# Two layers of mixers, woven tighter: one level and one softmax unit a round, four projections as a fourth thread, a shorter opening

## What is computed

```python
h = rmsnorm_2(x, norm1_g[l]); u = h @ w_in[l]        # 3648 columns
(mq, mk, mv, mo, mi, mf, aq, ak, av, hq, hf, hi, hg) = jnp.split(u, split_at, axis=-1)
y_m = mlstm_mixer(...)       # 4 heads of 64: silu(conv(q, k)), exp-gated scores, / max(|den|, exp(-m)), norm, * sigmoid(mo)
y_a = diff_attention(...)    # 4 heads x 2: softmax(q0 k0) - lam * softmax(q1 k1), times v, norm
y_h = hgrn2_mixer(...)       # 4 heads of 64: gated linear attention with per-channel decay, norm, * silu(hg)
x = x + concat(y_m, y_a, y_h) @ w_out[l]
x = x + square(relu(rmsnorm_2(x, norm2_g[l]) @ w_up[l])) @ w_down[l]
```

## Time and profile before

| what | value |
|---|---|
| median of three runs | 2468.59 us |
| the profiled execution | 2469.0 us, its span 2467.2 us |
| PE / DVE / ACT busy | 93% / 64% / 56% of the span |
| chain that ended last | PE 66%, DVE 16%, ACT 11%, DMA 6% |
| granted PE clock, mean | 0.964 of 2.4 GHz |
| opening, then mixers, of the first such layer | 1650.7 to 1677.4 us, 1677.4 to 1842.7 us |
| the same of the second | 2062.7 to 2089.0 us, 2089.0 to 2253.0 us |

### The profile page before, as it was taken

The page is one execution under the profiler, slowest core; times in us unless marked ns, Lnnn a source line. Parts: engine busy times, 40 slices in busy tenths (PEclk is TensorE's granted clock), DMA queues, the critical chain, the costliest instruction groups (busy, mean ns, idle before and its releaser), DMA issues.

```text
span 2467.2 us, 38778 instructions
## 1 busy us (share of the span) xinstructions
PE 2291.2 (93%) x16290; PEld 2119.9 (86%) x16290; DVE 1577.4 (64%) x2235; ACT 1377.3 (56%) x1910; POOL 19.9 (1%) x14
## 2 busy tenths in 40 slices
PE   7989999999999899998999999999669999877999
PEld 6979998999999799997888888788559998756999
DVE  4666555666575665463888888867646665754765
ACT  5754546544566554554777777766444444654443
POOL 0000000000000000000000000000000000000000
PEclk9999999999999899997999999999879999988999
DMA  6531234555454213341888888954114564412453
GB/s 230 155 110 52 95 104 145 171 175 186 156 166 158 92 52 103 112 158 70 315 297 300 302 307 307 313 186 137 57 35 145 180 197 146 140 35 77 163 188 137
DMA packets 111205, 398.12 MB, mean 161 GB/s; under 512 B 12336, under 2 KB 12336, under 8 KB 110768
## 3 DMA queue, kind: packets, MB, share of 16 engines
q1 hardware_dynamic: 111024, 395.58, 48.1%
HBM read 394.48 MB, written 1.05 MB: 160 GB/s over the span
## 4 chain that ended last, share of the span: by engine, by line
PE 66%; DVE 16%; ACT 11%; DMA 6%; issue 2%; SPq 0%; DVEq 0%; ACTq 0%
PE ps L413 65%; DVE wlo L2008 7%; DMA raw<-stream 5%; ACT whi L1234 4%; ACT arena L1244 3%; DVE arena L2008 2%; DVE arena L2016 1%; DVE scr L2008 1%; ACT scr L1244 1%; ACT arena_r L1244 1%; DVE h L2008 1%; DMA CO<-const 1%; ACT L1244 1%; ACT rst L1244 1%; DVE scr L2016 0%
## 5 line engine op out<-in xcount | busy, mean ns | idle before, releaser
L2008 DVE TENSOR_TENSOR wlo<-raw,whi 128x1024 fp32r<-128x1024 f32 (+1 forms) x762 | 901.6, 1197 | 552.0 <-ACT whi L1234 542.2
L1234 ACT ACTIVATE whi<-raw 128x1024 fp32r<-128x1024 f32 (+1 forms) x762 | 781.3, 1035 | 347.3 <-PE ps L413 268.0
L413 PE MATMUL ps<-uh,whi 128*128 128x256 f32 (+1 forms) x2240 | 654.3, 292 | 13.9 <-ACT scr L1244 6.2
L413 PE MATMUL ps<-ul,whi 128*128 128x256 f32 (+1 forms) x2240 | 635.4, 284 | 0.0
L413 PE MATMUL ps<-uh,wlo 128*128 128x256 f32 (+1 forms) x2240 | 635.0, 284 | 0.0
L413 PE MATMUL ps<-arena_r,whi 128*128 128x256 f32 x2720 | 491.3, 283 | 19.7 <-DVE arena_r L2008 12.3
L413 PEld LDWEIGHTS ps<-uh,whi 128*128 128x128 f32 (+1 forms) x2240 | 429.7, 192 | 25.9 <-issue 17.4
L413 PEld LDWEIGHTS ps<-arena_r,whi 128*128 128x128 f32 x2720 | 420.0, 190 | 24.5 <-DVE arena_r L2008 13.4
L413 PEld LDWEIGHTS ps<-ul,whi 128*128 128x128 f32 (+1 forms) x2240 | 429.9, 192 | 6.0 <-issue 5.2
L413 PEld LDWEIGHTS ps<-uh,wlo 128*128 128x128 f32 (+1 forms) x2240 | 429.4, 192 | 0.0
L413 PE MATMUL ps<-arena_r,wlo 128*128 128x256 f32 x1360 | 381.9, 281 | 0.0
(11 more groups left out here) (163 smaller groups left out, 1902.5 us busy)
## 6 DMA issues: line engine op xcount, KB each, us to landing
raw<-stream SPq DMA_DIRECT2D x694, 512.0 KB, 4.1
raw<-stream SPq DMA_DIRECT2D x64, 384.0 KB, 4.2
CO<-const SPq DMA_DIRECT2D x1, 2305.0 KB, 13.2
h<-xT SPq DMA_DIRECT2D x1, 1024.0 KB, 5.8
raw<-stream SPq DMA_DIRECT2D x4, 256.0 KB, 2.6
out<-h SPq DMA_DIRECT2D x4, 256.0 KB, 2.2
arena<-pT SPq DMA_DIRECT2D x2, 256.0 KB, 3.9
SM<-small SPq DMA_DIRECT2D x1, 464.0 KB, 3.2
```

Of the source, the lines that this page charges most:

```text
L413: return self.e.matmul(o, l, r, start=start, stop=stop, skip_group_check=True)
L1234: self.e.activation(M.whi[:, b:b + n], M.raw[:, a:a + n], ACT.Copy).then_inc(K.sem("weight_hi"), 1)
L2008: return self.e.tensor_tensor(o, a, b, op)
```

## The change

1. **Opening.** `mv` and `hv` leave it. PE: three sums, one `av` piece, the fourth sum, two `av` pieces, `columns`, the last `av` piece. ACT and DVE call `ahead` four times fewer there; `odd_values` is gone.
2. **Filler thread**, first in every round, on all three engines, with PSUM bank 2 alone (`mlstm` keeps 0 and 1). It idles for 8 beats, then has one piece a beat: `hv` 8 and 9, `mv` 10 and 11, `mo` 12 and 13, `hg` 14 and 15. `hv` and `mv` now use `u1` (no scaling) and one bank for both token tiles.
3. **mlstm** starts two beats earlier and no longer holds `mo`. PE: gates 2, `mc` 4 to 7, `mac` and `mE` 8, `mE` 9, `ms` 10 and 11, `md`, `me`, `mn` 12, `fin` 14. ACT and DVE keep step.
4. **attention**: projections in 1 to 8 as before, `normed` in 4, 6, 8, 10; then `softmax_beats`: scores of units 0 to 3 in beats 11 to 14, transposes in 12 to 15 (after the next unit's scores), `ao` in 14 and 16, `fin` in 15 and 17. DVE has the maximum (`most`) in 11 to 14 and `shares` in 12 to 15, ACT the exponentials in 11 to 14: the same beats as PE.
5. **hgrn**: level -1 in beat 5, level n in beat 6+n on PE and DVE both (DVE: product n, merge n-1, difference for n+1), decays of n+1 on ACT in the same beat; `ho` 14, `fin` 15.

No product, sum or copy of the mixers is left out; only the scaling by the column goes. The last beat of a stage is 17 in place of 34. The core of the diff:

```diff
-MLSTM = 4
+MLSTM = 2
+FILL = 8
+def softmax_beats(result, steps):
+    units, norms = [(h, qt) for h in (0, 2) for qt in range(2)], []
+    for n in range(8):
+        for x in norms:
+            next(x, None)
+        if n in (3, 5):
+            norms.append(result(n - 3))
+            next(norms[-1])
+        for late, step in steps:
+            if 0 <= n - late < 4:
+                step(*units[n - late])
+        yield
 # Tensor
+    def filler(self, l):
+        work, s = self.ring((2,)), self.mark("tensor_filler")
+        yield from idle(FILL)
+        yield from self.pair_values(work, s, ("hv", l), "w_in_2", l, 3080)
+        yield from self.pair_values(work, s, ("mv", l), "w_in_2", l, 512)
+        yield from self.proj_T(work, s, ("mo", l), "w_in_2", l, 768, 256)
+        yield from self.proj_T(work, s, ("hg", l), "w_in_2", l, 3336, 256)
 # Tensor.opening
+        end = self.values(*end, end=True)
+        if not first:
+            next(end)
         self.wait_ge(self.K.sem("const"), 16)
         self.sums(tag, range(4) if start else (3,))
-        for n, _ in enumerate(self.values(*end, end=True)):
-            if n == 0:
-                self.columns(tag)
+        for _ in range(1 if first else 2):
+            next(end)
+        self.columns(tag)
+        for _ in end:
+            pass
 # Tensor.attention
-        for h in (0, 2):
-            yield from heads(h)
+        yield from softmax_beats(result, ((0, score), (1, turn)))
 # Scalar.attention: ((1, turned), (0, exps)); Vector.attention: ((1, shares), (0, most))
 # Tensor.hgrn
         for lev in range(8):
-            yield
-            yield
             self.wait_ge(*K.when("hqk", l, lev))
             ...
             yield
-            if lev == 3:
-                yield from self.proj_T(work, s, ("hg", l), "w_in_2", l, 3336, 256)
 # Vector.hgrn
-        scores(-1)
-        yield
             ...
             self.tt(v3(x, 512), v3(B["hqk"], 512), wide(E, 512, 2), MUL).then_inc(*s("hqk", l, lev))
+            scores(lev - 1)
             if lev < 7:
                 decays(lev + 1)
             yield
-            yield
-            if lev < 7:
-                scores(lev)
-            yield
 # Tensor, Scalar, Vector .layer_b
-        weave([self.mlstm(l), self.attention(l), self.hgrn(l)])
+        weave([self.filler(l), self.mlstm(l), self.attention(l), self.hgrn(l)])
```

More of the change, by code:

```diff
@@ L243, in weave, with idle @@
                 live.remove(th)
[L246 to L251, removed]
-            yield
+def idle(n):
+    for _ in range(n):
+        yield
[10 more added lines that the diff above has]
+                step(*units[n - late])
+        yield
 def beside(thread, other, k):
@@ L483, in values, with pair_values @@
             yield
+    def pair_values(self, work, s, tag, name, l, c0):
+        b = self.bank(work, *tag)
+        for k0 in (0, 4):
+            i, wt = self.piece(name, l, k0, 4, c0, T)
+            for t in range(2):
+                for k in range(4):
+                    self.wait_ge(*self.K.when(*self.u_ready(k0 + k)))
+                    last = self.mm3(b[:, t * T:(t + 1) * T], pick(self.U, ALL, k0 + k, slice(t * P, t * P + P)),
+                                    pick(wt, ALL, k, ALL), k0 + k + t == 0, k0 + k == 7)
+            last.then_inc(*s(("used", i), *([("ps", *tag)] if k0 else [])))
+            yield
     def sums(self, tag, qs):
@@ L1069, in mlstm @@
         b = self.bank(work, "mn", l)
-        for t in range(2):
-            self.wait_ge(*K.when("mv", l, t))
+        self.wait_ge(*K.when("mv", l))
         for pt in range(2):
@@ L1128, in heads, with turn, result @@
+        def turn(h, qt):
+            nk = (qt + 1) * P
+            b = self.bank(work, "at", l, h, qt)
+            for z in range(2):
+                self.wait_ge(*K.when("ap", l, h + z, qt))
+                for j in range(qt + 1):
+                    last = self.e.transpose(b[:, z * nk + j * P:z * nk + (j + 1) * P], pa[z][:, j * P:(j + 1) * P], M.ident)
+            last.then_inc(*s("ps", "at", l, h, qt))
+        def result(h):
             b = self.bank(work, "ao", l, h)
@@ L1798, in mlstm @@
         self.act(B["E"], B["E"], ACT.Exp).then_inc(*s("mE1", l))
[L1799 to L1806, removed]
+        yield from idle(3)
         x = self.take(scr, "mem", l)
@@ L1935, in hgrn @@
             yield
[L1936 to L1951, removed]
+        for z in range(2):
+            self.wait_ge(*K.when("ps", "hs", l, 7, z))
+            self.act(v3(B["ST"][:, z * 1024:(z + 1) * 1024], 512)[:, :, P:T], v3(self.bank("hs", l, 7, z))[:, :, 0:P],
+                     ACT.Copy).then_inc(*s(("hst", l, z), ("free", "hs", l, 7, z)))
         self.wait_ge(*K.when("ps", "ho", l))
@@ L2040, in opening @@
         K, M, s, U = self.K, self.M, self.main, self.M.U
-        for _ in range(4):
+        short = tag[0] == "n1"
+        for _ in range(1 if short else 4):
             self.ahead()
@@ L2062, in low @@
                     SUB).then_inc(*s(("u1", tag, q), ("free", "nu", tag, q), *([("free", "rs", tag)] if q == 3 else [])))
-        self.ahead()
+        for _ in range(2 if short else 1):
+            self.ahead()
         self.wait_ge(*K.when("rs", tag))
@@ L2070, in opening @@
         scaled(3)
[L2071 to L2074, removed]
+        for q in (1, 2):
+            if not short:
+                self.ahead()
+            low(q)
         low(3)
@@ L2812, in hgrn @@
+        yield from softmax_beats(lambda h: self.group_norm(s, l, 2 + h, 2, gs), ((1, shares), (0, most)))
     def hgrn(self, l):
```

218 lines of the change are left out of this document (98 added, 120 removed).

## The result

The changed kernel takes **2502.56 us** (median of four, 2500.11 to 2504.10), the kernel before 2467.82 (median of four on the same chip): ratio 1.0139, 95% interval 1.0126 to 1.0152. It is slower by 1.4%. The forecast was 2490, in a range of 2446 to 2510. The profiled execution took 2500.11, its span is 2498.2 against 2467.2: 31.0 us more.

The account below looks back on a forecast made before the run. Chains across engines, plus PE's half clock, bound the mixers. Per layer: opening -10.7, from the first `u1` product +20.7 (121 + 49 + 16 against 165.3), later resume 0.7; both layers +21.4 on 2469.0 gave 2490 us, range 2446 to 2510.

Parts of the forecast that it names:

- The mechanism: Mixers from beat 6: PE's level waits for DVE's same-beat product and merge, behind that beat's mlstm and attention steps.
- The waits, beat by beat: PE's waits in mixer beats 6 to 17, priced one by one: together 49 us of idle in place of 40.
- The clock: Half-rate PE after waits in the mixers: 16 us a layer lost in place of 15, bounds 8 and 25.
- The opening: Before the first `u1` product: four pieces leave, `u1` wait 2.3 us; -10.7 us a layer, bounds -11.5 and -8.
- The table loads: ACT, beats 7 and 8: one more pair, 2 x 1.28 us, mostly inside beat 7's wait; no drain added.
- Slower still: Rival: clock drop in nearly every mixer beat, 25 us, with the forecast's waits; 2508 us, chance 0.15.
- Covered: Rival: mixer waits are covered, idle 36 us and 8 lost to the clock; 2448 us, chance 0.28.
- Even: Rival: idle plus rate loss 51 to 58 us, opening pays for denser beats; 2469 within 7, chance 0.17.

Follow-up runs that it names:

- Run 1: The changed kernel with PE's hgrn levels one beat behind DVE's product: 2442.27 us, ratio to the kernel before 0.9891.
- Run 9: The changed kernel with DVE alone issuing hgrn's product and merge ahead of attention's step, PE's beats unchanged: 2464.12 us, ratio to the kernel before 0.9979.
- Run 4: The changed kernel with spare PE products, six ahead of level 0's wait and four ahead of level 1's: 2497.75 us, ratio to the kernel before 1.0106.
- Run 2: The changed kernel with the opening's PSUM banks turned so that attention's first projection meets a free one: 2502.85 us, ratio to the kernel before 1.0135.
- run 6: The kernel before with one hgrn level a beat, product and level in the same beat, `hg` after level 7: 2528.39 us, ratio 1.0244.
- run 7: The kernel before with `softmax_beats` on all three engines, levels still three beats apart: 2465.43 us, ratio 0.9987.
- 12: The kernel before with one hgrn level a beat, PE a beat behind DVE and ACT, softmax units still spaced: 2506.83 us, ratio 1.0152.
- run 8: The changed kernel with PE's levels one beat behind DVE's product and `mv` and `hv` back in the opening: 2435.23 us, ratio to the kernel before 0.9867.
- run 3: The changed kernel with `mv` and `hv` back in the opening, filler with `mo` and `hg` only: 2492.76 us, ratio to the kernel before 1.0096.

## Why the prediction was right, and where it was off

- **The mechanism** was the forecast's: each beat from 6 on a chain from DVE's mlstm or attention step over product and merge to PE's level. Run 1 gives that distance back and the 60 us go. Run 9 shows which part of the chain weighed most.
- **The waits, beat by beat.** Forecast for beats 6 to 10: 6.1, 4.1, 4.7, 3.4, 4.8; measured 6.3, 4.6, 5.4, 3.4, 4.8. Beat 12: 1.3, 1.3 and 2.7; measured 1.2, 1.0 and 3.0. Beats 11 and 13: 2.9 and 2.2, measured 2.6 and 2.2; `ho` 4.2, measured 3.7; the last transposes 5.8, measured 5.7. The sum was 49, and idle was 48.3 in both layers. That it fits within a microsecond is in part luck: the last `fin` and the output product were forecast at 5.7 and took 3.7, which covers the 1.4 missing in beats 6 to 8 and a wait of 0.7 in beat 14 that wasn't forecast.
- **The clock.** Forecast 16 us a layer; by the same count 19.1 and 20.4. The failed step is "2 us lost in eight of the beats, since dense pieces follow and some waits are short": there are 11 stretches at 0.50 in the first layer (47.8 us, 39.8 us of PE's work in them). Ten stand at the waits of beats 6 to 15, one in each; the eleventh is the start of the mixers, behind the opening's wait of 4.16. Run 4 shows two that cost 2.3 and 2.1 us. So it was the number of drops that was too low, not their size. This is 7.5 us of the gap. The prediction also passed over two low slices of the earlier trace rows, an 8 and a 7 in the first pair of layers; they bear on nothing here.
- **The opening.** Forecast -10.7; measured -7.9 and -10.6. The failed step is "only the last `av` piece stands between `columns` and the first use of `u1`": a PSUM bank stands there too, held until ACT's `diff_values`. The wait was 4.16 and 2.70, against the 2.3 taken. Run 2 shows the bank, and behind it waits for `u1` of 1.9 and 1.1, less than the 2.3. This is 2.9 us of the gap. (The prediction read the first `u1` product of before at 1677.4; it starts at 1676.47, which moves 0.9 us from opening to mixers.)
- **The table loads** were in the sum with their 1.28 us and nothing more. The timeline of ACT in beat 7 of the changed kernel:

```profile
1726.47 0.84 ACT L1275 ACTIVATE arena<-ps,SM 128x256 f32<-128x256 f32 x2 [3.85 <-PE ps L426]
1727.33 1.28 ACT L1275 ACT_TABLE_LOAD   x1
1728.63 0.63 ACT L1275 ACTIVATE arena<-arena 128x512 f32<-128x512 f32 x1
```

  The next activation starts 0.02 us after the load, as in the earlier trace rows. The drain of 1.38 us that the Trainium skill states ("ScalarE: Activation LUTs", What ACT_TABLE_LOAD costs) shows in no row here: the activation ahead of this load ends 0.02 us before it, so there is no gap on either side.
- **Sum.** The forecast was 21.4 us more, the two spans differ by 31.0. Of the 9.6 between them the clock is 7.5 and the openings 2.9, less 1.4 for idle time; the other 0.6 lies in the marks of before and in the rest of the program. Of the 12.6 between 2490 and the median, these 9.6 are the larger part; 2.5 are that the profiled execution is the fastest of its four, and 0.4 the step from 2490.4 to 2490.
- **The rivals.** "Slower still" needed 25 us a layer at the clock; 19 and 20 lie between its figure and the forecast's 16. Its price of 2508 is nearer to the 2502.6 measured than the forecast's 2490 is, and the forecast's own range ended at 2503. The rule behind it, the Trainium skill's ("TensorE: Matmul & The Clock Gate", on HAM oscillation), is that every step ending in a wait pays the restart. The trace agrees with it: all ten beats from 6 to 15 start a stretch at 0.50 behind their wait, where I had eight. It put the size too high: 1.7 us a stretch were lost (19.1 over 11), where "slower still" had 2.5 a beat. "Covered" said that idle and clock together decide at 51 us; with run 1's slack they are 39, and the kernel is faster. Its price, 2448, fits that version and not this one. "Even" fell with 67 us.
- **What my theory still had wrong** shows in runs 6, 7 and 12, missed by 48, 19 and 41 us. I priced each mixer's edit as if the other stayed its cover. The three fit with this, argued and not shown by itself: what counts is how many mixers still run beside each other, and the one left alone waits for its own chain, at a clock of 0.67 in the window of run 6.

**Left open:** what a shorter opening is worth when its banks are turned and the sums' bank is left where it was; where the 20 us that run 7 missed lie; and a beat of slack for the softmax, which needs a second buffer for its shares and wasn't tried. PE's waits ahead of the transposes are still 4.1 us in run 8, the last one 3.5.

## What to carry to other kernels

Engines that feed each other through in-order streams want a beat between producer and consumer: work put into the same beat waits for everything that stands in front of it on the producer's engine, and here that distance was worth 60 us of 2500 with not one instruction added. Shorten threads that cover each other together, since one that ends early uncovers another. A piece put at the head of a beat doesn't fill the wait that follows it in the same stream (run 3). And before moving work out of a dense stage, or turning the banks, ask for every user which PSUM bank it takes and who is still reading it.

## What I had not expected of the hardware

- The cost of the clock goes neither with the number of drops nor with the idle time. Five stretches at 0.50 cost 15 us before the change, eleven cost 19 after it, seven cost 27 in run 6; idle times of 23 us (run 8) and 41 us (before) go with the same 15. What it follows is the work of PE inside the stretches, half of which is lost: 30.7, 39.8 and 56.6 us of work in the three kernels.
- Spare products in a wait do bring a level back to 1.24 us from 2.21, but of the 9.5 us that the two layers' four beats gain, 5 reach the median.
